# Moving the weight slots and the FFN activations of a two-block transformer kernel by 64 and 128 bytes in SBUF

## The chip, the core and the metric

The kernel runs on one core of a Trainium2 chip. The metric is the device time in microseconds of one execution. Three executions of the kernel before took 1388.61, 1388.72 and 1394.03 us; their median, 1388.72 us, is the time before.

## What is computed

Two transformer blocks run one after the other on 512 tokens with 1024 features, all in fp32. What matters here are the linears, the products of an activation with a weight matrix; everything between them is named only.

```python
def first_block(x, c, ctx, ...):                 # one layer
    h  = modulate(rmsnorm(x), shift, scale)      # 512 x 1024
    hc = modulate(rmsnorm(ctx), ...)             # 256 x 1024
    z  = h @ w_in                                # q, k, v, gate and conv inputs
    kvc = hc @ w_in[:, ATT_W:3 * ATT_W]          # keys and values of the context
    y  = concat(neighbourhood attention, spatial gating, conformer conv) @ w_out
    x  = x + mod[2] * y
    h2 = modulate(rmsnorm(x), ...)
    gate, up = split(h2 @ w_up)                  # 2 x 2816 columns
    x  = x + mod[5] * ((silu(dwconv(gate)) * up) @ w_down)

def second_block(x, ...):                        # one layer
    proj = rms_norm(x) @ w_in                    # q, k, v, conv inputs, gates
    merged = sigmoid(g_att) * (stick_breaking(q, k, v) @ w_att) \
           + sigmoid(g_conv) * (conv branch @ w_conv)
    x = x + rms_norm(merged @ w_out)
    a, g = split(causal_dwconv(rms_norm(x) @ w_up))   # 2 x 2816 columns
    return x + rms_norm((gelu(g) * a) @ w_down)
```

## The kernel before

Activations lie in SBUF with the features on the 128 partitions: `h_hi[:, k, :]` holds the features 128 k to 128 k + 127 of all 512 tokens. Each fp32 operand of a linear is split into a high and a low part in the type fp32r, and a product is three matmuls that add up in one PSUM bank: high weight by high activation, low weight by high activation, high weight by low activation. `product` (with `with_high`, L586 and L587, and `with_low`, L590) issues them. A block of 128 output features is a loop of `product` over the 8 (or, down in the FFNs, 22) chunks of 128 input features. In the trace these matmuls have the lines L586, L587 and L590, whoever calls.

In the call `e.matmul(dst, lhs, rhs)` the second operand is stationary: an instruction of its own, LDWEIGHTS, loads its 128 columns into the array. The third is the moving operand, streamed through with 512 columns, or 256 where half of the tokens are done at a time. In nearly all linears the weight is stationary and the activation moves. It is the other way round where the values are computed with tokens on the partitions: `values_high` and `values_low` (L750, L753, L761) at the start of block one, and the loop over `W["v2"]` in block two (through `product`). There the weight moves.

The weights pass through three slots. SyncE loads a tile of 128 x 1024 fp32 to `raw_w`; ScalarE rounds it to `w_hi` (L1347), and VectorE subtracts to get `w_lo` (L1916). From the second out-projection to the start of the second FFN six further slots, `late_hi` and `late_lo`, are in use as well. The order of the matmuls on TensorE is written out by hand (`mixer_order`, `stick_order`, then plain loops), and so is the order on the other engines; semaphores couple them. Each engine runs its list in order.

The tiles are laid into SBUF one after another in the order of the `sb(...)` lines in `two_blocks`. An inner `with` gives its room back at its end, so the tiles of different stages share addresses. A tile starts at the next multiple of 32 bytes. The first, `x_res`, starts at 16512 bytes of each partition, which is 128 modulo 256. All chunks within the tiles below are whole multiples of 512 bytes apart, so a tile's start modulo 256 is also that of each operand taken from it. Starts, in bytes of a partition:

| tile | stage | start before | modulo 256 |
|---|---|---|---|
| `h_hi`, `h_lo` | all | 32896, 49280 | 128, 128 |
| `raw_w`, `w_hi`, `w_lo` | all | 82752, 95040, 107328 | 64, 64, 64 |
| `hc_hi`, `hc_lo` | mixer of block one | 190176, 198368 | 224, 224 |
| `a_hi`, `a_lo` | first FFN, down | 123904, 168960 | 0, 0 |
| `att_hi`, `att_lo`, `cnv_hi`, `cnv_lo` | merge of block two | 119680, 127872, 136064, 144256 | 128 |
| `m_hi`, `m_lo` | second out-projection | 168832, 185216 | 128, 128 |
| `late_hi`, `late_lo` | between the stages of block two | 119680, 144256 | 128, 128 |
| `a2_hi`, `a2_lo` | second FFN, down | 119680, 164736 | 128, 128 |
| `sp_hi`, `sp_lo`, `minus` | sums of the stick-breaking attention | 203648, 213888, 224128 | 128 |

The trace names both `a_hi` and `a2_hi` as `a_hi`; the first stands at 521 to 646 us, the second at 1254 to 1378 us.

Of the kernel before, what the change touches and what calls it, by code (L numbers as in the profile page):

```python
# [13 lines left out]
P = 128  # L14
D = 1024
KC = D // P
# [25 lines left out]
EPS = 1e-6  # L42
NEG = -1e30
SLOT = 1024


COLUMN_SIZES = [
# [45 lines left out]
class Loads:  # L93
# [5 lines left out]
    def row(self):  # L99
        self.load.append(("row", self.io["ada_rows"][self.n_rows, :, :], SLOT, self.n_rows))  # L100
        self.n_rows += 1
# [171 lines left out]
def two_blocks(nc, io, out):  # L273
    with ExitStack() as whole:
        def sb(stack, name, shape, dt=F32):
            return stack.enter_context(nc.sbuf_tensor(name, shape, dt))
# [19 lines left out]
        both_gains = sb(whole, "both_gains", [P, KC])  # L296
        std = sb(whole, "std", [P, 2 * TT])
        rstd = sb(whole, "rstd", [P, 2 * TT])
        raw = sb(whole, "raw_w", [P, RAW, SLOT])
        w_hi = sb(whole, "w_hi", [P, KEPT, SLOT], F32R)  # L300
        w_lo = sb(whole, "w_lo", [P, KEPT, SLOT], F32R)
        silu_c = sb(whole, "silu_c", [P, KC, 2])
        banks = whole.enter_context(nc.psum_tensor("banks", [P, 8, T], F32))
        bank = [banks[:, b, :] for b in range(8)]
        score_banks, turned_banks = banks[:, 0:2, :], banks[:, 2:4, :]
# [1 line left out]
        with ExitStack() as modulated:  # L307
            silu_row = sb(modulated, "silu_row", [P, D])
            mod_raw = sb(modulated, "mod_raw", [P, 4 * KC])
            with ExitStack() as mixer:  # L310
                mods = sb(mixer, "mods", [P, KC, 4])
                gains = sb(mixer, "gains", [P, KC, 2])
                k_loc = sb(mixer, "k_loc", [P, AC, T])
                k_ctx = sb(mixer, "k_ctx", [P, AC, CTX])
                v_loc = sb(mixer, "v_loc", [P, CBLK, ATT])
                cv_acc = sb(mixer, "cv_acc", [P, CC, T])
                stats = sb(mixer, "stats", [P, 5 * TT])
                sg_square = sb(mixer, "sg_square", [P, SG])
                cv_scratch = sb(mixer, "cv_scratch", [P, CC, T])
                soft = sb(mixer, "soft", [P, 2, 6])  # L320
                group_std = sb(mixer, "group_std", [P, CC * TT * 2])
                group_factor = sb(mixer, "group_factor", [P, CC * TT * 2])
                with ExitStack() as beginning:
                    early = sb(beginning, "early", [P, 6, 2, SLOT])
                q_loc = sb(mixer, "q_loc", [P, AC, T])
                v_mid = sb(mixer, "v_mid", [P, CBLK - 1, ATT])
                v_ctx = sb(mixer, "v_ctx", [P, CT, ATT])
                sg_out = sb(mixer, "sg_out", [P, SC, T])
                sg_v = sb(mixer, "sg_v", [P, TT, SG])
                cv_in = sb(mixer, "cv_in", [P, CC, T + 2 * PAD])  # L330
                sg_small = sb(mixer, "sg_small_sb", [P, SC * P + 2 * SG + 4 * P])
                hc_hi = sb(mixer, "hc_hi", [P, KC, CTX], F32R)
                hc_lo = sb(mixer, "hc_lo", [P, KC, CTX], F32R)
                with ExitStack() as context:
                    xc = sb(context, "xc", [P, KC, CTX])
                with ExitStack() as attention:
                    biased = sb(attention, "biased", [P, 2, len(SPAN_OFFS), 2, SPAN // GROUP, ROWS, GROUP])
                    probs_more = sb(attention, "probs_more", [P, 2, T])
            with ExitStack() as ffn:
                a_hi = sb(ffn, "a_hi", [P, FC, T], F32R)  # L340
                a_lo = sb(ffn, "a_lo", [P, FC, T], F32R)
        with ExitStack() as branch:
# [20 lines left out]
        with ExitStack() as between_stages:  # L363
            late_hi = sb(between_stages, "late_hi", [P, LATE_KEPT, SLOT], F32R)
            late_lo = sb(between_stages, "late_lo", [P, LATE_KEPT, SLOT], F32R)
# [2517 lines left out]
```

## Time and profile before

| | |
|---|---|
| time, median of three | 1388.72 us |
| the profiled execution, first to last instruction (span) | 1387.9 us |
| TensorE busy with matmuls | 1358.3 us, 98% |
| TensorE loading weights (beside the matmuls) | 1123.6 us, 81% |
| VectorE busy | 757.9 us, 55% |
| ScalarE busy | 604.9 us, 44% |
| mean DMA rate | 108 GB/s |
| mean granted TensorE clock | 0.995 of full |

The profile gives the span of the execution that it was taken on, not that execution's own device time; the span is 0.8 us below the median of the time. A matmul that follows another begins before the first one has ended, so the busy time of a group of matmuls, and the mean of one, hold an overlap. How fast a stretch of matmuls goes is read from their starts: the start of the last less the start of the first, by the number of steps between them.

### The profile page before, as it was taken

Reading aid. Unit: us, or ns where it says so; the run is one execution under the profiler, and the core shown is the slowest. Engines: PE = TensorE matmul, PEld = TensorE weight load, DVE = VectorE, ACT = ScalarE, POOL = GpSimd, SP = SyncE. Lnnn points to the kernel's source line nnn. Section 1 sums busy time; section 2 is a strip of 40 time slices with the busy share of each in tenths; the row PEclk is TensorE's granted clock in tenths of the full one; section 3 lists DMA queues with packets and bytes.
Section 4 is the critical chain, followed back from the end, with each engine's and each line's share of the span. In section 5 each row is a group of like instructions: output and inputs, shape, how many; then the busy total and the mean of one; then the engine's idle time right before and its main releaser. Section 6 shows DMA issues by size and latency. Waiting matters only on the chain.

```text
span 1387.9 us, 17388 instructions
## 1 busy us (share of the span) xinstructions
PE 1358.3 (98%) x7040; PEld 1123.6 (81%) x7040; DVE 757.9 (55%) x1070; ACT 604.9 (44%) x866; POOL 4.0 (0%) x11
## 2 busy tenths in 40 slices
PE   5999999999999999999999999999999999999997
PEld 3787877888888888889888888788998788888887
DVE  5679866775554442336414444345777756663224
ACT  5647778453333333224344454334534434443221
POOL 0000000000000000000000000000000000000000
PEclk9999999999999999999999999999999999999998
DMA  9734322414433232332222211234302332223331
GB/s 378 279 129 147 141 73 75 145 64 150 160 113 106 91 95 90 87 107 78 97 86 76 77 61 54 77 103 144 126 1 91 107 103 95 91 87 101 96 97 61
DMA packets 43102, 150.45 MB, mean 108 GB/s; under 512 B 4752, under 2 KB 6928, under 8 KB 41872
## 3 DMA queue, kind: packets, MB, share of 16 engines
q1 hardware_dynamic: 42144, 144.76, 31.2%
q0 software_dynamic: 880, 4.59, 1.0%
q8 instruction: 56, 0.92, 0.3%
q14 instruction: 22, 0.18, 0.0%
HBM read 146.45 MB, written 2.10 MB: 107 GB/s over the span
## 4 chain that ended last, share of the span: by engine, by line
PE 91%; DVE 5%; ACT 2%; issue 1%; DMA 0%; SPq 0%; ACTq 0%; DVEq 0%
PE banks L586 27%; PE banks L587 26%; PE banks L590 26%; DVE w_lo L1916 1%; PE banks L893 1%; ACT w_hi L1347 1%; PE banks L750 1%; PE banks L753 1%; PE banks L761 1%; PE banks L876 1%; PE banks L1157 1%; PE banks L1156 1%; PE banks L1148 1%; PE banks L1184 1%; PE banks L723 1%
## 5 line engine op out<-in xcount | busy, mean ns | idle before, releaser
L586 PE MATMUL banks<-h_hi,w_hi 128*128 128x512 f32 (+1 forms) x1248 | 472.9, 381 | 1.9 <-DVE w_lo L1916 1.3
L587 PE MATMUL banks<-h_hi,w_lo 128*128 128x512 f32 (+1 forms) x1248 | 466.5, 375 | 0.0
L590 PE MATMUL banks<-h_lo,w_hi 128*128 128x512 f32 (+1 forms) x1248 | 461.0, 376 | 0.9 <-DVE h_lo L2271 0.2
L1916 DVE TENSOR_TENSOR w_lo<-raw_w,w_hi 128x1024 fp32r<-128x1024 f32 (+2 forms) x221 | 256.3, 1162 | 321.5 <-ACT w_hi L1347 319.5
L1347 ACT ACTIVATE w_hi<-raw_w 128x1024 fp32r<-128x1024 f32 (+2 forms) x221 | 221.5, 1004 | 231.8 <-PE banks L590 213.4
L586 PEld LDWEIGHTS banks<-h_hi,w_hi 128*128 128x128 f32 x1248 | 234.5, 188 | 50.3 <-issue 6.1
L590 PEld LDWEIGHTS banks<-h_lo,w_hi 128*128 128x128 f32 x1248 | 230.9, 188 | 48.8 <-DVE h_lo L2271 1.9
L587 PEld LDWEIGHTS banks<-h_hi,w_lo 128*128 128x128 f32 x1248 | 234.6, 188 | 40.9
L586 PE MATMUL banks<-a_hi,w_hi 128*128 128x512 f32 (+1 forms) x396 | 146.2, 369 | 0.0
L587 PE MATMUL banks<-a_hi,w_lo 128*128 128x512 f32 (+1 forms) x396 | 146.2, 369 | 0.0
L590 PE MATMUL banks<-a_lo,w_hi 128*128 128x512 f32 (+1 forms) x396 | 145.2, 367 | 0.0
L586 PEld LDWEIGHTS banks<-a_hi,w_hi 128*128 128x128 f32 x396 | 74.4, 188 | 13.8
L590 PEld LDWEIGHTS banks<-a_lo,w_hi 128*128 128x128 f32 x396 | 74.4, 188 | 13.5
L587 PEld LDWEIGHTS banks<-a_hi,w_lo 128*128 128x128 f32 x396 | 74.6, 188 | 12.8
L1985 DVE SCALAR_TENSOR_TENSOR exact<-banks,cols_sb,exact 128x510 f32<-128x510 f32 (+1 forms) x44 | 32.9, 748 | 38.1 <-ACT exact L1873 37.3
L1985 DVE SCALAR_TENSOR_TENSOR normed<-banks,cols_sb,normed 128x510 f32<-128x510 f32 (+1 forms) x66 | 49.2, 746 | 0.8
L1362 ACT ACTIVATE a_hi<-normed 128x512 fp32r<-128x512 f32 x44 | 27.8, 632 | 46.1 <-DVE normed L2332 29.4
L1979 DVE SCALAR_TENSOR_TENSOR cv_acc<-cv_in,cols_sb,cv_acc 128x512 f32<-128x512 f32 x60 | 45.0, 749 | 1.2
L1873 ACT ACTIVATE exact<-banks,cols_sb 128x512 f32<-128x512 f32 x22 | 15.1, 685 | 59.9 <-PE banks L590 59.9
L1646 ACT ACTIVATE normed<-normed 128x512 f32<-128x512 f32 x22 | 13.9, 632 | 54.7 <-DVE normed L2328 54.7
L2440 DVE SCALAR_TENSOR_TENSOR sp<-banks,sp 128x1024 f32<-128x1024 f32 (+1 forms) x8 | 11.9, 1492 | 41.5 <-ACT sp L1738 41.5
L1877 ACT ACTIVATE exact<-exact 128x512 f32<-128x512 f32 x22 | 13.9, 632 | 44.2 <-DVE exact L1985 44.2
(315 smaller groups left out, 1513.7 us busy)
## 6 DMA issues: line engine op xcount, KB each, us to landing
raw_w<-in_w_ffn_up SPq DMA_DIRECT2D x44, 512.0 KB, 3.4
raw_w<-in_w_up SPq DMA_DIRECT2D x44, 512.0 KB, 3.4
raw_w<-in_ada_rows SPq DMA_DIRECT2D x24, 512.0 KB, 3.9
early<-in_ada_turned SPq DMA_DIRECT2D x8, 1024.0 KB, 16.8
raw_w<-in_w_gates SPq DMA_DIRECT2D x16, 512.0 KB, 3.2
raw_w<-in_w_ffn_down SPq DMA_DIRECT2D x16, 448.0 KB, 3.3
raw_w<-in_w_down SPq DMA_DIRECT2D x16, 448.0 KB, 3.3
raw_w<-in_w_conv SPq DMA_DIRECT2D x12, 512.0 KB, 3.3
```

The costliest lines, as they stand in the source:

```text
L586: e.matmul(dst, lhs_hi, rhs_hi, start=first, stop=False)
L587: e.matmul(dst, lhs_lo, rhs_hi, start=False, stop=False)
L590: return e.matmul(dst, lhs_hi, rhs_lo, start=False, stop=last)
L723: done = e.matmul(bank[b][32 * part:32 * part + 2, 0:2 * P], silu_c[:, 2 * m + part // 2, :], tiles[:, half, part * 2 * P:(part + 1) * 2 * ...
L1347: e.activation(hi[:, 0:n], raw[:, i % RAW, 0:n], ACT.Copy).then_inc(s_hi, 1)
L1362: e.activation(dst, src, ACT.Copy).then_inc(done, 1)
L1646: e.activation(y, y, ACT.Silu).then_inc(s_up_silu, 1)
L1873: e.activation(dst, bank[b[n]][:, :], ACT.Copy, scale=col("conv_ffn_w_2", w)).then_inc(s_up2_centre.sem, 1)
L1877: e.activation(y, y, ACT.Gelu_apprx_tanh).then_inc(s_up2_gelu.sem, 1)
L1916: e.tensor_tensor(lo[:, 0:n], raw[:, i % RAW, 0:n], hi[:, 0:n].bitcast(F32), ALU.subtract).then_inc(s_lo, 1)
L1979: e.scalar_tensor_tensor(out=acc, in0=src, scalar=col("cv_w", i), in1=acc, op0=ALU.mult, op1=ALU.add).then_inc(s_tap_v, 1)
L1985: return e.scalar_tensor_tensor(out=y[:, shift:T], in0=src[:, 0:T - shift], scalar=w, in1=y[:, shift:T], op0=ALU.mult, op1=ALU.add)
```

## The change

The small tile `silu_c` (64 bytes) moves from behind `w_lo` to ahead of `raw_w`. Two tiles that nothing uses are put in as gaps: 160 bytes ahead of `hc_hi`, and 128 bytes ahead of `a_hi`. No instruction is added, removed or reordered on any engine; what differs are addresses.

```diff
+BEFORE_A, BEFORE_HC = 32, 40
...
         rstd = sb(whole, "rstd", [P, 2 * TT])
+        silu_c = sb(whole, "silu_c", [P, KC, 2])
         raw = sb(whole, "raw_w", [P, RAW, SLOT])
         w_hi = sb(whole, "w_hi", [P, KEPT, SLOT], F32R)
         w_lo = sb(whole, "w_lo", [P, KEPT, SLOT], F32R)
-        silu_c = sb(whole, "silu_c", [P, KC, 2])
...
                 sg_small = sb(mixer, "sg_small_sb", [P, SC * P + 2 * SG + 4 * P])
+                sb(mixer, "before_hc", [P, BEFORE_HC])
                 hc_hi = sb(mixer, "hc_hi", [P, KC, CTX], F32R)
                 hc_lo = sb(mixer, "hc_lo", [P, KC, CTX], F32R)
...
             with ExitStack() as ffn:
+                sb(ffn, "before_a", [P, BEFORE_A])
                 a_hi = sb(ffn, "a_hi", [P, FC, T], F32R)
                 a_lo = sb(ffn, "a_lo", [P, FC, T], F32R)
```

The tiles that start elsewhere after it:

| tile | start before, modulo 256 | start after, modulo 256 |
|---|---|---|
| `silu_c` | 119616, 64 | 82752, 64 |
| `raw_w` | 82752, 64 | 82816, 128 |
| `w_hi` | 95040, 64 | 95104, 128 |
| `w_lo` | 107328, 64 | 107392, 128 |
| `hc_hi`, `hc_lo` | 190176, 198368, 224 | 190336, 198528, 128 |
| `a_hi`, `a_lo` | 123904, 168960, 0 | 124032, 169088, 128 |
| `xc`, `biased` (share their room) | 206560, 224 | 206720, 128 |
| `probs_more` | 218848, 224 | 219008, 128 |

All other tiles stay where they are.

## Rows read from the trace of the kernel before

**Rows 1.** The page: the chain that ended last, share of the span by engine.
```profile
PE 91%; DVE 5%; ACT 2%; issue 1%; DMA 0%; SPq 0%; ACTq 0%; DVEq 0%
```

**Rows 2.** Groups by shape on TensorE: line, operation, output<-operands, xcount, busy us, mean ns.
```profile
L586 PE MATMUL banks<-h_hi,w_hi 128*128 128x512 f32 x1072 | 425.0, 396 | 0.8 <-DVE w_lo L1916 0.6 <-issue 0.2
...
L586 PE MATMUL banks<-a_hi,w_hi 128*128 128x512 f32 x308 | 121.3, 394 | 0.0
L586 PE MATMUL banks<-h_hi,w_hi 128*128 128x256 f32 x176 | 47.9, 284 | 1.1 <-DVE w_lo L1916 0.8 <-ACT h_hi L1609 0.3
```

**Rows 3.** Timeline of TensorE (start us, us long): first and last matmul, FFN up.
```profile
296.21 0.40 PE L586 MATMUL banks<-h_hi,w_hi 128*128 128x512 f32 x1
...
521.22 0.39 PE L590 MATMUL banks<-h_lo,w_hi 128*128 128x512 f32 x1
```

**Rows 4.** The same for the down-projection of the first FFN.
```profile
521.45 0.39 PE L586 MATMUL banks<-a_hi,w_hi 128*128 128x512 f32 x1
...
629.01 0.39 PE L590 MATMUL banks<-a_lo,w_hi 128*128 128x512 f32 x1
```

**Rows 5.** The same for the down-projection of the second FFN.
```profile
1254.67 0.39 PE L586 MATMUL banks<-a_hi,w_hi 128*128 128x512 f32 x1
...
1360.19 0.39 PE L590 MATMUL banks<-a_lo,w_hi 128*128 128x512 f32 x1
```

**Rows 6.** The same for the values of block two, where the weight moves.
```profile
694.72 0.39 PE L586 MATMUL banks<-w_hi,h_hi 128*128 128x512 f32 x1
...
716.89 0.40 PE L590 MATMUL banks<-w_lo,h_hi 128*128 128x512 f32 x1
```

**Rows 7.** Out-projection of block two: last stretch from `w_hi`, whole stretch from `late_hi`.
```profile
968.99 0.39 PE L586 MATMUL banks<-m_hi,w_hi 128*128 128x512 f32 x1
...
974.25 0.39 PE L590 MATMUL banks<-m_lo,w_hi 128*128 128x512 f32 x1
974.48 0.40 PE L586 MATMUL banks<-m_hi,late_hi 128*128 128x512 f32 x1
...
985.15 0.39 PE L590 MATMUL banks<-m_lo,late_hi 128*128 128x512 f32 x1
```

**Rows 8.** Start of the second FFN: a tile from `late_hi` at full width, first, tenth, last.
```profile
1039.58 0.40 PE L586 MATMUL banks<-h_hi,late_hi 128*128 128x512 f32 x1
...
1041.67 0.39 PE L586 MATMUL banks<-h_hi,late_hi 128*128 128x512 f32 x1
...
1044.84 0.39 PE L590 MATMUL banks<-h_lo,late_hi 128*128 128x512 f32 x1
```

**Rows 9.** Sums of the stick-breaking attention, full width, first and last of ten.
```profile
785.95 0.39 PE L1156 MATMUL banks<-sp_hi,minus 128*128 128x512 f32 x1
...
787.99 0.39 PE L1157 MATMUL banks<-sp_lo,minus 128*128 128x512 f32 x1
```

**Rows 10.** The chain at 55 to 60 us: values of block one (start us, us, what).
```profile
56.23 0.93 PE banks L753 x4
```

**Rows 11.** Half width, 256 columns: the out-projection of block two, from `late_hi`.
```profile
985.38 0.28 PE L586 MATMUL banks<-m_hi,late_hi 128*128 128x256 f32 x1
...
995.69 0.28 PE L590 MATMUL banks<-m_lo,late_hi 128*128 128x256 f32 x1
```

**Rows 12.** Half width, 256 columns: the down-projection of the first FFN, from `w_hi`.
```profile
629.24 0.28 PE L586 MATMUL banks<-a_hi,w_hi 128*128 128x256 f32 x1
...
638.66 0.28 PE L590 MATMUL banks<-a_lo,w_hi 128*128 128x256 f32 x1
```

**Rows 13.** The chain at 1039 to 1080 us, by line.
```profile
by line: DVE w_lo L1916 20.7%; DVE exact L1985 17.4%; DVE normed L1985 17.3%; ACT w_hi L1347 15.4%; DVE normed L2633 8.6%; issue 8.0%; ACT exact L1877 7.8%; PE banks L586 2.1%; PE banks L587 1.4%; PE banks L590 1.2%; ACTq L1872 0.3%; ACT a_
```

**Rows 14.** Instructions of one tile, `a_lo`: ns min/median/max, first and last start.
```profile
L2334 DVE TENSOR_TENSOR a_lo<-normed,a_hi x22: 691/693/694, 296.9 to 523.1; 128x512 fp32r<-128x512 f32 x22
L2635 DVE TENSOR_TENSOR a_lo<-normed,a_hi x22: 691/693/695, 1047.9 to 1259.2; 128x512 fp32r<-128x512 f32 x22
```

**Rows 15.** Windows: us, busy (x count) of PE, PEld, DVE, ACT, POOL, clock, DMA share, GB/s; mixer.
```profile
100.00:262.00 162.00, 158.58 (x1066) 126.14 (x1063) 123.23 (x187) 114.04 (x191) 1.06 (x2) 1.00 0.33 114
```

## The prediction, made before the changed kernel ran

> **What bounds the kernel now.** I read the page first. The chain that ended last lies on TensorE for 91% of the span [rows 1], and TensorE is busy 98% of it, VectorE 55% and ScalarE 44% (table above). So the time is, nearly everywhere, the number of matmuls times the step from one to the next. The mean duration of a matmul, 396 ns for `h_hi,w_hi` and 394 ns for `a_hi,w_hi` [rows 2], doesn't tell that step, since neighbours overlap; the timeline does. The reader is to take two starts far apart and divide by the number of steps between, counted from the loops.
>
> In the up-projection of the first FFN 984 matmuls of full width (41 tiles, 8 chunks, 3 products) start between 296.21 and 521.22 us: 225.01 / 983 = 228.9 ns a step [rows 3]. Directly after it, in the down-projection, 462 matmuls (7 blocks, 22 chunks, 3 products) take (629.01 - 521.45) / 461 = 233.3 ns [rows 4]. The down-projection of the second FFN, the same 462 matmuls of the same form, takes (1360.19 - 1254.67) / 461 = 228.9 ns [rows 5]. TensorE waits for nothing in any of them. By the table of starts the moving operand is at 0 modulo 256 in the slow one and at 128 in the fast ones, while the stationary weight is at 64 in all three. Where the weight itself moves, at 64, the step is slow too: (716.89 - 694.72) / 95 = 233.4 ns in the values of block two [rows 6] and 0.93 us for four, about 233 ns, in those of block one [rows 10]. So the start of the moving operand is worth 4.4 ns.
>
> The stationary operand seems to count as well. In the out-projection of block two the same `m_hi` and `m_lo`, at 128, move over weights first from `w_hi` at 64, (974.25 - 968.99) / 23 = 228.7 ns, and then over weights from `late_hi` at 128, (985.15 - 974.48) / 47 = 227.0 ns, its first step of 0.24 us included [rows 7]. The sums of the stick-breaking attention have both operands at 128 and go at (787.99 - 785.95) / 9 = 226.7 ns [rows 9]. The tile from `late_hi` at the start of the second FFN, both at 128 again, goes at (1044.84 - 1041.67) / 14 = 226.4 ns once it has settled, but its first nine steps took 232.2 ns each [rows 8].
>
> **The change, part by part.** No instruction is added or moved on any queue, so no wait changes its place. What changes is the start of some operands. I cost it against the profiled span of 1387.9 us, which is 0.8 us under the median; I take the differences off the median, 1388.72.
>
> Step after the change: every linear gets both operands at 128, the case of [rows 7 to 9]. I take 226.7 ns, the value of [rows 9], between the settled 226.4 and the 227.0 with its slow first step.
>
> (a) Weight stationary, moving operand already at 128, full width. Chunks: 1072 of `h` and 154 of `a2`, half of the 308 in [rows 2], and by the loops 32 of `att`, 32 of `cnv` and 24 of `m`, together 1314, or 3942 matmuls. Each goes from 228.9 to 226.7, 2.2 ns less. Two stretches are set apart. In the mixer of block one (176 of these chunks, 528 matmuls, worth 1.2 us) TensorE is busy 158.6 of 162 us, but softmax on ScalarE and VectorE (114 and 123 us busy) is part of the chain [rows 15]; short runs between small matmuls may also never settle. I take half, 0.6 us, between 0 and 1.2. From 1045 to 1079 us (34 / 0.2289 = about 149 matmuls, 0.3 us) the chain runs through VectorE and ScalarE, TensorE's lines having a few per cent [rows 13]: a faster TensorE only waits there, and I take nothing. The rest, 3942 - 528 - 149 = 3265, gives 3265 x 2.2 = 7.2 us.
>
> (b) First FFN, down-projection, full width: 462 x (233.3 - 226.7) = 3.0 us.
>
> (c) Values, where the weight moves: 96 matmuls in block two and 144 in block one: 240 x 6.6 = 1.6 us.
>
> (d) Half width. The step of `late_hi` in the out-projection is (995.69 - 985.38) / 86 = 119.9 ns [rows 11], that of `w_hi` in the first FFN (638.66 - 629.24) / 80 = 117.8 ns, with `a` at 0 [rows 12]. So here both at 128 is the slower pair, by 2.1 ns. 176 chunks of `h` [rows 2], 88 of `a` and 32 of `hc` by the loops are 888 matmuls: 888 x 2.1 = 1.9 us more. Between 0, if the half width of `late_hi` is slow for its own reasons, and 2.9 us, if some of the stretches go faster than the one shown.
>
> (e) ScalarE, VectorE and DMA. `a_lo` is written at 0 modulo 256 in the first FFN and at 128 in the second, in 691/693/694 and 691/693/695 ns [rows 14]. So VectorE doesn't see the phase, and I put `raw_w`, `w_lo` and `biased` at nothing. The loads run ahead of their use nearly everywhere; at most the 0.3 us stretch above could show a difference.
>
> Sum: 0.6 + 7.2 + 3.0 + 1.6 - 1.9 = 10.5 us. **Forecast: 1388.7 - 10.5 = 1378.2 us.** Its own ends: with the whole mixer and no half-width loss 13.0 us, 1375.7; with nothing in the mixer, 227.0 ns instead of 226.7 (4400 matmuls x 0.3 = 1.3 us) and 2.9 us lost at half width, 7.6 us, 1381.1.
>
> **The rivals.** *Only the moving operand counts.* The 2 ns between `w_hi` and `late_hi` would then belong to something else that the stretch of `late_hi` has, and full-width steps end at 228.9. What speaks for it is that the big, clean pair [rows 4, 5] shows only the moving operand, and that the slow opening in [rows 8] stands where both are at 128. Against it: in [rows 7] nothing but the weight's place changes from one matmul to the next, and [rows 9] agree in another stage. It gives (462 + 240) x 4.4 = 3.1 us: 1385.6.
>
> *Places don't matter at all*, the change doesn't do what it says: the 4.4 ns between the two down-projections would come from their stages (the FFNs differ in what ScalarE and VectorE do beside them), and the time stays at 1388.7. Against it, [rows 6, 10] are slow in two further stages and share only the place of their moving operand.
> The Trainium skill, page "TensorE: Matmul & The Clock Gate", section "Step-by-step: what each phase is for", says that TensorE has two independent read ports, so that loading the next weights takes nothing from the running matmul, and the page's step for 512 columns is 215.7 ns with no term for an address. By that rule, this rival holds. The trace doesn't bear it out: the same form takes 228.9 ns in one stage and 233.3 in another.
>
> *Slower: the slow opening lasts.* The first nine steps of [rows 8] have `h` moving at 128 over a weight at 128, which is just what 3216 matmuls (1072 chunks) become. If that pair keeps its 232.2 ns instead of settling, those lose 3.3 ns each, 10.6 us, and half width 1.9 us, against 462 x 1.1 = 0.5 us from (b), 240 x 1.1 = 0.3 us from (c) and 726 x 2.2 = 1.6 us from `a2`, `att`, `cnv` and `m`: 10.1 us slower, 1398.8. Between the two paces lie 3216 x 5.5 = 17.7 us, so it decides from a share of 10.5 / 17.7, about six in ten, of those matmuls at the slow pace. Against it: the opening follows directly on half-width matmuls, was over after nine steps, and the long runs in [rows 4, 5] hold one pace.
>
> **How the numbers follow.** Forecast 0.65; only the moving operand 0.15; no effect 0.09; slower 0.07; and 0.04 for a gain beyond my ends. The predicted time is that of the likeliest, 1378.2 us. The range holds the forecast's ends and the first rival, 1375.0 to 1386.5 us, and leaves out the others, 0.20 together. A measurement of this kernel can tell about 0.5%, 6.9 us, from no change, so faster is below 1381.8: the forecast and what lies beyond it, less a few cases at its upper edge, 0.69. Slower is above 1395.7, 0.07. The rest, 0.24, is within 0.5%.
>
> **What the profile of the changed kernel would show.** If I am right: the FFN up-projections go from 228.9 to about 226.7 ns a step, the two down-projections become equal, also at 226.7 (the first from 233.3), the values of block two likewise, the half-width stretches go to about 119.9, and `late_hi` stays where it is. The stretch 1045 to 1079 us keeps its length, with TensorE waiting a little more. The forecast is wrong if `h` over `w` stays at 228.9 (the first rival) or goes to 232 (the last), if the first down-projection stays at 233.3 (places don't matter), or if the steps shorten and the span doesn't, with new waits of TensorE for `w_lo`.

## The result

The changed kernel took 1380.94 us, the median of six executions between 1378.10 and 1383.61, against 1389.81 us (1386.97 to 1394.03) for the kernel before, measured beside it. The ratio is 0.9936, with a 95% interval of 0.9917 to 0.9955: 8.9 us faster. Put on another chip later, beside the kernel before again, it took 1377.98 us against 1389.00, a ratio of 0.9919 (0.9905 to 0.9932), 11.0 us faster. The forecast was 1378.2 us, 10.5 us faster.

The profiled execution of the changed kernel took 1383.48 us, at the slow end of its six, with a span of 1382.2 us. Its page has the same number of instructions, and TensorE is busy for 5.4 us less than before:

```profile
span 1382.2 us, 17388 instructions
## 1 busy us (share of the span) xinstructions
PE 1352.9 (98%) x7040; PEld 1129.3 (82%) x7040; DVE 757.4 (55%) x1070; ACT 604.8 (44%) x866; POOL 4.0 (0%) x11
```

The lines that answer to [rows 3 to 7] are in the timeline of TensorE of the changed kernel (start us, us long, line, operands). All line numbers are three higher than before. First and last matmul of the first FFN's up-projection, of its down-projection, of the values of block two, and of the second FFN's down-projection:

```profile
295.68 0.40 PE L589 MATMUL banks<-h_hi,w_hi 128*128 128x512 f32 x1
...
518.52 0.39 PE L593 MATMUL banks<-h_lo,w_hi 128*128 128x512 f32 x1
518.75 0.39 PE L589 MATMUL banks<-a_hi,w_hi 128*128 128x512 f32 x1
...
623.25 0.39 PE L593 MATMUL banks<-a_lo,w_hi 128*128 128x512 f32 x1
```
```profile
688.96 0.39 PE L589 MATMUL banks<-w_hi,h_hi 128*128 128x512 f32 x1
...
710.49 0.39 PE L593 MATMUL banks<-w_lo,h_hi 128*128 128x512 f32 x1
```
```profile
1249.73 0.39 PE L589 MATMUL banks<-a_hi,w_hi 128*128 128x512 f32 x1
...
1354.22 0.39 PE L593 MATMUL banks<-a_lo,w_hi 128*128 128x512 f32 x1
```

The steps are 222.84 / 983 = 226.7 ns (before 228.9), 104.50 / 461 = 226.7 (233.3), 21.53 / 95 = 226.6 (233.4) and 104.49 / 461 = 226.7 (228.9). All four have become the step of the sums of stick-breaking [rows 9]. Half width went the other way, to the step of [rows 11]; the first FFN's down-projection again, which answers to [rows 12], now takes 9.59 / 80 = 119.9 ns instead of 117.8:

```profile
623.47 0.28 PE L589 MATMUL banks<-a_hi,w_hi 128*128 128x256 f32 x1
...
633.06 0.28 PE L593 MATMUL banks<-a_lo,w_hi 128*128 128x256 f32 x1
```

Cut at the starts of the stages, and at the end at the first of TensorE's last four matmuls (1379.38 and 1373.69 us), the two traces give this ledger, in us:

| stage | before | after | difference |
|---|---|---|---|
| start, values of block one | 66.33 | 65.92 | -0.41 |
| mixer of block one | 196.21 | 195.87 | -0.34 |
| end of out-projection, norm, start of up (half width) | 33.67 | 33.89 | +0.22 |
| first FFN, up | 225.24 | 223.07 | -2.17 |
| first FFN, down, full width | 107.79 | 104.72 | -3.07 |
| its end and norm (half width) | 36.19 | 36.41 | +0.22 |
| queries and keys of block two | 29.29 | 29.08 | -0.21 |
| values, stick-breaking, conv | 180.86 | 179.26 | -1.60 |
| merge | 82.40 | 81.60 | -0.80 |
| second out-projection, full width | 27.40 | 27.24 | -0.16 |
| its end, output norm (half width) | 22.31 | 23.89 | +1.58 |
| output norm, start of up (half width) | 31.89 | 35.38 | +3.49 |
| second FFN, up | 215.09 | 213.40 | -1.69 |
| second FFN, down, full width | 105.74 | 104.72 | -1.02 |
| end (half width) | 18.97 | 19.24 | +0.27 |
| sum | 1379.38 | 1373.69 | -5.69 |

The sum agrees with the spans, 1387.9 and 1382.2 us. Two stages got longer by 5.1 us together, and most of that isn't the places. There the granted clock fell to half, 1.2 of 2.4 GHz. The windows of the kernel before, then of the changed one (us; busy us and instructions of PE, PEld, DVE, ACT, POOL; granted clock; DMA):

```profile
998.00:1002.00 4.00, 4.00 (x22) 4.00 (x23) 1.56 (x8) 1.32 (x4) 0.00 (x0) 0.57 0.01 4
```
```profile
990.00:996.00 6.00, 6.00 (x29) 6.00 (x30) 2.40 (x10) 1.32 (x4) 0.00 (x0) 0.50 0.01 3
1007.00:1013.00 6.00, 6.00 (x29) 6.00 (x29) 4.63 (x18) 1.57 (x5) 0.00 (x0) 0.50 0.01 3
```

The kernel before had one fall of 3.4 us there, the changed one two of 6.8 us. Executions without one show the stages undisturbed: `w_only` (below), with the weights at 128, takes 20.82 and 32.34 us in them, `a_only`, with the weights at 64, 31.89 us in the second. So the falls cost 22.31 - 20.82 = 1.5 us before and (23.89 - 20.82) + (35.38 - 32.34) = 6.1 us after, and the places themselves cost 0.45 us. Without the clock's part the ledger sums to -5.69 - (6.1 - 1.5) = -10.3 us. Executions at the same mean granted clock say nearly the same. On the chip of the second comparison, at 0.995, three of the changed kernel took 1377.85 to 1378.56 us and eleven of the kernel before 1387.94 to 1389.80, their medians 10.8 us apart.

### The profile page after: what moved, and what is told of

It reads as the page before. It is cut to its first block, busy times and chain, and to the rows that moved or that the text cites. A ratio compares the mean times of both kernels' runs of the same rounds, so it can differ in the third digit from the quotient of the medians.

```text
span 1382.2 us, 17388 instructions
## 1 busy us (share of the span) xinstructions
PE 1352.9 (98%) x7040; PEld 1129.3 (82%) x7040; DVE 757.4 (55%) x1070; ACT 604.8 (44%) x866; POOL 4.0 (0%) x11
## 4 chain that ended last, share of the span: by engine, by line
PE 91%; DVE 5%; ACT 2%; issue 1%; DMA 0%; SPq 0%; ACTq 0%; DVEq 0%
PE banks L589 27%; PE banks L593 26%; PE banks L590 26%; DVE w_lo L1919 1%; PE banks L896 1%; ACT w_hi L1350 1%; PE banks L879 1%; PE banks L764 1%; PE banks L756 1%; PE banks L753 1%; PE banks L1160 1%; PE banks L1159 1%; PE banks L726 1%; PE banks L1151 1%; PE banks L1187 1%
```

## The experiments

Twelve runs, on three chips, each beside the kernel before: ten kernels, and once more the change and `after_spread`. `w_96`, `w_160` and `w_lo_off` have two executions each, the others four to twelve.

| kernel | median, us | before, us | ratio (95%) | moving less stationary, modulo 256: `h` over `w`, `a` over `w` |
|---|---|---|---|---|
| `w_only` | 1380.75 | 1389.34 | 0.9935 (0.9913, 0.9957) | 0, 128 |
| `a_only` | 1387.26 | 1389.34 | 0.9980 (0.9968, 0.9992) | +64, +64 |
| `hc_only` | 1388.74 | 1389.34 | 0.9990 (0.9979, 1.0000) | +64, -64 |
| `all_at_192` | 1380.63 | 1389.34 | 0.9925 (0.9901, 0.9949) | 0, 0 |
| `w_96` | 1405.94 | 1389.60 | 1.0117 (1.0092, 1.0142) | +32, -96 |
| `w_160` | 1405.25 | 1389.60 | 1.0112 (1.0089, 1.0135) | -32, +96 |
| `after_spread` | 1377.97 | 1389.60 | 0.9916 (0.9900, 0.9931) | 0, 0 |
| `before_spread` | 1387.10 | 1389.60 | 0.9984 (0.9974, 0.9994) | +64, -64 |
| `before_plus_64` | 1389.01 | 1389.00 | 1.0001 (0.9992, 1.0010) | +64, -64 |
| `w_lo_off` | 1404.74 | 1389.00 | 1.0111 (1.0093, 1.0130) | 0 and -32, 0 and -32 |
| `after_again` | 1377.98 | 1389.00 | 0.9919 (0.9905, 0.9932) | 0, 0 |
| `after_spread_again` | 1377.00 | 1389.00 | 0.9910 (0.9897, 0.9924) | 0, 0 |

### Each part of the change alone

`w_only` is the kernel before with `silu_c` moved:

```diff
+        silu_c = sb(whole, "silu_c", [P, KC, 2])
         raw = sb(whole, "raw_w", [P, RAW, SLOT])
...
-        silu_c = sb(whole, "silu_c", [P, KC, 2])
```

> Only the three weight slots move, from 64 to 128 modulo 256; hc stays at 224 and a at 0. If the weight's place counts (my theory), h over w goes from 228.9 to 226.7 ns a step at full width, the second down-projection likewise, the values with the weight moving from 233.3 to 226.7, half width from 117.8 to 120, and the time falls by 7.2 + 0.6 + 1.6 - 1.9 = 7.5 us before what a does. The first down-projection, a at 0 over w at 128, is a pair not seen yet: 233.3 if the moving operand off 128 is slow whatever the weight does, 226.7 if the weight alone sets it. If only the moving operand counts, h over w stays at 228.9 and the time falls by about 1 us.

Measured: 8.6 us faster. `h` over `w` steps at 226.7 ns (983 steps in 222.85 us), the second down-projection at 226.7. The pair that no trace had shown, `a` at 0 over `w` at 128, stayed slow, (626.51 - 518.95) / 461 = 233.3 ns:

```profile
518.95 0.40 PE L586 MATMUL banks<-a_hi,w_hi 128*128 128x512 f32 x1
...
626.51 0.39 PE L590 MATMUL banks<-a_lo,w_hi 128*128 128x512 f32 x1
```

So the weight's place counts, and most of the gain is in this one 64-byte move: not all of the 8.6 us, though. The profiled execution of `w_only` has no fall of the clock in the output norms, the one of the kernel before has one, worth 1.5 us. Stage by stage, without that, the two traces are 7.1 us apart, where 7.5 were expected. The rival "only the moving operand counts" falls: no `h` moved here.

`a_only` has just the gap ahead of `a_hi`:

```diff
+                sb(ffn, "before_a", [P, 32])
                 a_hi = sb(ffn, "a_hi", [P, FC, T], F32R)
```

> Only a_hi and a_lo move, from 0 to 128; the weight slots stay at 64. By my theory the first down-projection becomes the pair of the second, 228.9 ns a step instead of 233.3: 462 x 4.4 = 2.0 us faster, and all other stretches stay as before. If what slows the first down-projection is its stage and not its place, it stays at 233.3.

As expected, the first down-projection stepped at (628.70 - 523.18) / 461 = 228.9 ns, the step of the second [rows 5], and the time fell by 2.1 us:

```profile
523.18 0.39 PE L587 MATMUL banks<-a_hi,w_hi 128*128 128x512 f32 x1
...
628.70 0.39 PE L591 MATMUL banks<-a_lo,w_hi 128*128 128x512 f32 x1
```

That settles the rival "places don't matter": the stage is the same, the place alone changed. The Trainium skill (page "TensorE: Matmul & The Clock Gate", section "Step-by-step: what each phase is for") says that loading the next weights takes nothing from the running matmul, and it has no cost for an address. Such a cost is there: one and the same stage steps at 228.9 or at 233.3 ns by where its operands lie. Whether it is the weight load that disturbs the matmul, no run here shows.

`hc_only` has just the gap ahead of `hc_hi`:

```diff
+                sb(mixer, "before_hc", [P, 40])
                 hc_hi = sb(mixer, "hc_hi", [P, KC, CTX], F32R)
```

> Only hc_hi and hc_lo move, from 224 to 128 (and xc, biased and probs_more with them). By my theory hc over w at half width, some 96 matmuls at 117.4 ns a step, stays within 3 ns of that, the values with the context stay at 233.3 because their weight still moves at 64, and the time doesn't move: within 0.5 us of before. If the softmax is sensitive to the place of biased or probs_more, the mixer (100 to 262 us) changes by over 0.5 us.

The two medians are 0.6 us apart, which the interval (0.9979 to 1.0000) can't tell from nothing. As expected, `hc` over `w` at half width stays within 3 ns (117.8 ns a step, 117.4 before), and the values with the context stay at 233.4. In the trace the mixer is 0.06 us longer, the start 0.08 and the end 0.09 us shorter, and every other stage is within 0.02 us. The softmax didn't notice.

### Is it the place, or the distance?

In the traces before these runs every fast pair had both operands at 128. `all_at_192` is the whole change plus a gap of 64 bytes ahead of the first tile, so that everything starts at 192.

```diff
+        sb(whole, "before_x", [P, 16])
         x = sb(whole, "x_res", [P, KC, T])
```

> All that the change does, and every tile of the kernel 64 bytes further: the operands of all linears start at 192 modulo 256. If only the distance between the moving and the stationary operand counts (my theory, formed on the traces: distance 0 gives 226.7), every full-width stretch goes at 226.7 ns and half width at 120, as at 128, and the time is that of the change, some 9 to 10 us below before. If 128 itself is the good place of the moving operand (0 and 64 were slow), the full-width stretches go at 229 to 233 ns, and the time is at or above that of before.

It steps at (517.60 - 294.76) / 983 = 226.7 ns, and the time is that of the change:

```profile
294.76 0.40 PE L589 MATMUL banks<-h_hi,w_hi 128*128 128x512 f32 x1
...
517.60 0.39 PE L593 MATMUL banks<-h_lo,w_hi 128*128 128x512 f32 x1
```

The number 128 has nothing to it; what counts is that moving and stationary operand start at the same place modulo 256. `before_plus_64` is the same test for the pair +64: the kernel before with the gap of 64 bytes ahead of `x_res` and nothing else.

> The kernel before with every tile 64 bytes further: h at 192, the weight slots at 128, a at 64 modulo 256, all distances as before. If only the distance counts (my theory), every stretch repeats before: h over w 228.9 ns a step (+64), the first down-projection 233.3 (-64), the values 233.3, and the time is that of before within 1 us. If the places themselves count, h at 192 over w at 128 gives another step than 228.9; after all_at_192 only the pair +64 is open to this.

It repeats before: 1389.01 against 1389.00 us, and 228.9, 233.3 and 228.9 ns in the three FFN stretches.

### The other distances

`w_96` and `w_160` put the weight slots 32 bytes to either side of `h`. Gaps ahead of and behind the slots add up to 256 bytes, so that the tiles behind keep their places modulo 256; `a` stays at 0.

```diff
+        silu_c = sb(whole, "silu_c", [P, KC, 2])
+        sb(whole, "before_w", [P, 56])        # w_160: [P, 8]
         raw = sb(whole, "raw_w", [P, RAW, SLOT])
...
+        sb(whole, "behind_w", [P, 8])         # w_160: [P, 56]
```

> The weight slots start at 96, h, att, cnv, m and a2 at 128, a at 0 modulo 256: distances of the moving from the stationary operand of +32 and, for a, +160 (which is -96). If the step grows with the distance to either side (my theory), h over w lies between 226.7 and 228.9 ns, and a over w near 233.3. If only an equal start gives 226.7 and every other one is a step of its own, h over w is at 228.9 or 233.3. Half width: 120 if it goes with 226.7, 113 to 118 if not. Time between that of w_only, about 8 us below before, and before.

> The weight slots start at 160, h and the others at 128, a at 0 modulo 256: distances of -32 and, for a, +96. By my theory h over w lies between 226.7 (distance 0) and 233.3 (distance -64), and a over w between 228.9 and 233.3. If a positive distance is always 228.9 and a negative one always 233.3, h over w is at 233.3, so that the time rises by some 3942 x 4.4 = 17 us over before, and a over w is at 228.9.

My theory, a step that grows with the distance, fell. 32 bytes off is as bad as 128: `h` over `w` steps at (528.17 - 298.80) / 983 = 233.3 ns in `w_96` (below), and at 233.3 in `w_160` too. The time rose by 16 us in both, 3942 matmuls by 4.4 ns being 17.

```profile
298.80 0.40 PE L588 MATMUL banks<-h_hi,w_hi 128*128 128x512 f32 x1
...
528.17 0.39 PE L592 MATMUL banks<-h_lo,w_hi 128*128 128x512 f32 x1
```

Together, full width, by the distance of the moving from the stationary operand modulo 256:

| distance | step, ns | seen in |
|---|---|---|
| 0 | 226.7 | the change, `w_only`, `all_at_192`, [rows 7, 9] |
| +64 | 228.9 | [rows 3, 5], `a_only`, `before_plus_64` |
| +32, -32, +96, 128 | 233.3 | `w_96`, `w_160`, `w_only` |
| -64 | 233.3 | [rows 4, 6], `before_plus_64` |
| -96 | 234.3 | `w_96`, first FFN down |

These are the long runs; short ones between other matmuls go 1 to 3 ns slower. 256 is the period as far as these kernels show: `m_hi` less `late_hi` is 49152 bytes, a multiple of 512, `w_hi` less `h_hi` in the change 62208, an odd multiple of 256, and both pairs step at 226.7 ns, while a distance of 128 gave 233.3. So the kernel before stood, with most of its matmuls, at the second-best distance. Why +64 is better than the others I can't say.

`w_lo_off` asks whether each matmul pays for its own pair. It is the whole change with 32 bytes between `w_hi` and `w_lo`, and 224 behind.

```diff
         w_hi = sb(whole, "w_hi", [P, KEPT, SLOT], F32R)
+        sb(whole, "before_w_lo", [P, 8])
         w_lo = sb(whole, "w_lo", [P, KEPT, SLOT], F32R)
+        sb(whole, "behind_w", [P, 56])
```

> The whole change, but w_lo alone starts at 160 modulo 256, 32 bytes off the activations; w_hi stays at 128. A distance of 32 bytes gave 233.3 ns a step with both halves of the weight off. If each matmul pays for its own pair of operands (my theory), one in three pays: (2 x 226.7 + 233.3) / 3 = 228.9 ns a step, and the time is some 9 us above the change. If one pair out of place upsets the whole stream, all steps are at 233.3. If the rounding is coarser than one matmul, it stays at 226.7.

I was wrong: with one weight in three off, the mean step is that of all three off, (526.90 - 297.54) / 983 = 233.3 ns, and the time is 15.7 us above before. One step of 233.3 after two of 226.7 would have given 228.9. The single steps in that stretch are 239, 229 and 232 ns in turn, so none of the three kept 226.7.

```profile
297.54 0.40 PE L590 MATMUL banks<-h_hi,w_hi 128*128 128x512 f32 x1
...
526.90 0.40 PE L594 MATMUL banks<-h_lo,w_hi 128*128 128x512 f32 x1
```

In this stream one operand in three out of place was enough for the full loss. It isn't so everywhere: in the values of block two of the same trace, where the weight moves, the 95 steps took 22.02 us, 231.8 ns each, between the two. What in the chip does this the runs don't show.

Half width has no such clean table. Distance 0 gives 119.9 ns in the long runs; the others gave 116.8 (+32), 117.4 (-96), 117.8 (-64 and +64), 118.4 (-32), 118.8 (128) and, as slow as distance 0, 120.0 (+96: 80 steps in 9.60 us in `w_160`). And at +64 one stretch, the first 66 half-width matmuls at the end of the second down-projection, took 117.8 ns a step in the kernel before and (1365.94 - 1358.57) / 65 = 113.4 ns in `a_only`, where that stage is the same:

```profile
1358.57 0.28 PE L587 MATMUL banks<-a_hi,w_hi 128*128 128x256 f32 x1
...
1365.94 0.28 PE L591 MATMUL banks<-a_lo,w_hi 128*128 128x256 f32 x1
```

### The clock in the output norms

In the output norms TensorE adds up squares over the partitions: a row of matmuls with one column, 2.6 us long, twice (L1227, at 996 and 1011 us of the kernel before). Of the eleven profiles of kernels that have these rows in one piece, nine show the clock falling 2.2 to 4.1 us after the start of one of them; `w_only` and `a_only` don't. `after_spread` deals the row out: the running totals are summed ahead, the last parts behind, with a product between any two pieces.

```diff
+            def output_piece(half, what, last_part):
...
+                part = (parts_of if last_part else totals)[what]
...
-                    if (u, j) == (KC, 4):
-                        output_sums(0)
+                    if u == KC and 1 <= j <= 6:
+                        output_piece(0, (j - 1) % 3, j >= 4)
...
-            side_by_side_halves(0, tiles, ..., {1: output_sums, 5: output_spreads})
+            side_by_side_halves(0, tiles, ...,
+                                {(0, 1): output_pieces((CROSS, False), (SCALED_SQUARES, False)),
+                                 (1, 0): output_pieces((Y_SQUARES, False), (Y_SQUARES, True)),
+                                 (1, 1): output_pieces((CROSS, True), (SCALED_SQUARES, True)), 5: output_spreads})
```

`before_spread` is the kernel before with the same edit. Both ran once, and the change with and without it once more.

> The whole change, and the sums over partitions of the output norms (24 matmuls of one column in a row, 2.6 us, twice) are dealt out in pieces of 0.4 to 0.9 us between the products around them. The granted clock fell to half 1 to 3 us after such a row in the traces of before (998 to 1002 us) and of the change (989 to 997 and 1006 to 1014 us), and the stretch of the output norms was 1.5 us longer for the first and 6.1 us for the second than in executions without it. If the rows of one-column matmuls bring the clock down (my theory), the clock stays at 1.00 from 985 to 1035 us, the runs lie close together at 1377.0 to 1378.5, and the median is 2 to 4 us below that of the change. If the clock falls for another reason, the median stays at 1380.9 and the runs spread over 5 us as before.

> The kernel before with its one-column matmuls dealt out in the same way. By my theory the clock stays at 1.00 in the output norms and the median falls by 2 us to about 1387.0, with runs close together; the difference to after_spread is then the change without the clock's part: by stage the two traces give 10.7 us. If the change costs clock drops that the kernel before does not have, the difference of these two is larger than that of the change and before (8.9 us); if the drops have nothing to do with it, it is the same 8.9 us.

> The change once more, beside after_spread_again on the same chip: median 1380.9, runs in groups at 1378, 1381 and 1383.5 us by how often the clock fell in the output norms.

> The change with its one-column matmuls dealt out, once more, for the interval: 1377 to 1379 us, below after_again by 2 to 4 us. If the first run of it was luck, the two have the same median.

In all three profiles with the edit the clock stays at 1.00 through the output norms. Windows of `after_spread_again`, then of `after_again`, which has the row in one piece:

```profile
977.00:998.00 21.00, 21.00 (x179) 20.96 (x179) 14.50 (x37) 9.56 (x23) 0.00 (x0) 1.00 0.18 62
998.00:1030.00 32.00, 32.00 (x272) 32.00 (x271) 22.94 (x67) 8.71 (x20) 0.00 (x0) 1.00 0.01 1
```
```profile
976.00:997.00 21.00, 21.00 (x179) 20.96 (x179) 15.38 (x39) 9.56 (x23) 0.00 (x0) 1.00 0.21 73
997.00:1030.00 33.00, 33.00 (x268) 33.00 (x267) 22.83 (x67) 8.63 (x20) 0.00 (x0) 0.95 0.00 1
```

The kernel before fell by 2.5 us, from 1389.60 to 1387.10, as expected. `after_spread` took 1377.97 us, its four between 1377.12 and 1378.75: 3.0 us below the change's 1380.94, but that was on another chip. The five executions of `after_spread_again` lie between 1376.53 and 1377.31 us, close together as expected. But `after_again` didn't repeat the 1380.9 that I expected: its four lie between 1377.32 and 1378.56, so the edit was worth 1.0 us on that chip, not 2 to 4. How often the clock falls differs between sets of executions, and the edit doesn't end all falls: four of twelve executions of `before_spread` were at 1388.9 to 1389.5 us and a clock of 0.994, the other eight at 1386.2 to 1387.7 and 0.997 or 0.998. No profile caught one of the four, so where their clock fell is open. The output norms aren't the only place: in all but one profile (`before_spread`) it is at half for 3.4 or 6.8 us between 20 and 29 us, and in `a_only` for 3.4 us at 208 us, right after 16 matmuls of two columns (205.9 to 207.9 us), which made the mixer 1.6 us longer.

Between the two kernels with the edit, on one chip, the change is worth 1387.10 - 1377.97 = 9.1 us; between the two without, 8.9 and 11.0 us by chip. My expectation that the 8.9 of the first comparison would either stay or grow can't be decided by these numbers: `after_spread` had a mean clock of 0.995 or 0.996, most of `before_spread` 0.997. At the same clock, 0.997, four executions of `after_spread_again` and seven of `before_spread` have medians 10.1 us apart, though on two chips. The 10.7 us in that expectation came of cutting the last stage at the fourth of four matmuls before and at the first of them after; cut alike, it is 10.3. The best version is the change with the rows dealt out, 1377.00 us, 0.9910 (0.9897 to 0.9924) of before.

## Why the prediction was right

The forecast, 1378.2 us, lies 2.7 us below the first median and 0.2 us above the one of `after_again`; the way, the mechanism and most terms were right. That the sum of 10.5 us comes so near to the ledger's 10.3 is partly luck: (d) charged 0.7 us too much, and (c) and the mixer promised 0.8 us too much.

- **What bounds the kernel**: right. The time followed the step of the matmuls, stage by stage, and no new wait appeared. What the prediction took for the place of the moving operand ("worth 4.4 ns") is its distance from the stationary one: `all_at_192` and `before_plus_64` show that the place doesn't matter.
- **(a) Weight stationary**: expected 7.2 us outside the mixer. The ledger has 2.17 + 0.21 + 0.80 + 0.16 + 1.69 + 1.02, and of the 1.60 the 0.96 that aren't values: 7.0 us. The 226.7 ns came from the nine steps of [rows 9], between 226.4 and 227.0 in 14 and 47 others [rows 8, 7], and held for thousands. In the mixer I took 0.6 us, and 0.34 came. The stretch that I left out kept its length: it ends with TensorE's wait for `w_lo`, which grew by what TensorE had gained. Before and after (the idle time in brackets):

```profile
1078.76 0.50 PE L586 MATMUL banks<-h_hi,w_hi 128*128 128x512 f32 x1 [0.57 <-DVE w_lo L1916]
```
```profile
1075.49 0.50 PE L589 MATMUL banks<-h_hi,w_hi 128*128 128x512 f32 x1 [0.90 <-DVE w_lo L1919]
```

  From the `late_hi` tile of [rows 8] to that wait's end it is 1078.76 - 1039.58 = 39.18 us before and 1075.49 - 1036.33 = 39.16 after.
- **(b) First down-projection**: expected 3.0 us, 3.07 came.
- **(c) Values**: in block two 95 steps went from 22.17 to 21.53 us, 0.64 as expected. In block one I had 1.0 us and the two traces show 0.41. Its last 72 matmuls gained 0.47 us, as priced (from 49.54 to 66.33 us before, from 49.60 to 65.92 after); the earlier ones, in pieces between others, show no gain in these two traces, with the clock at half for 3.4 us in both. That stage starts behind the first loads and varies: it ends at 64.9 to 66.1 us in the traces with the weights in line with `h` and at 65.4 to 66.5 in those with them at the distance of before. The averages, over six and five traces, are 0.6 us apart.
- **(d) Half width**: mis-sized. The step was right, 119.9 ns, but I charged 2.1 ns for all 888 matmuls, 1.9 us. The ledger has +0.22, +0.22, (without the clock) +0.45 and +0.27, 1.2 us. Many of these matmuls stand side by side with a norm and wait for their inputs, and there the longer step is hidden, just as the shorter one was in the stretch above: the 45 from 272 us and the 102 from 282 us on go at 153.3 and 139.8 ns a step before and at 153.1 and 140.3 after. I hadn't taken those off.
- **(e) Other engines**: right. `a_lo` in the changed kernel takes 691/693/695 ns in the first FFN, as in [rows 14].
- **The slow opening** [rows 8] stayed an opening: the runs of 984 matmuls hold 226.7.

What the sum didn't have is the clock. I worked from differences of steps at full clock, which give the 10.3 us of the ledger. The times of the first set go with the clock: 1378.1 and 1378.2 us at a mean of 0.995, 1380.9 and 1381.0 at 0.993, 1383.5 and 1383.6 at 0.991 and 0.990, and their median is one at 0.993: against the 10.3 to 10.8 us at an equal clock, 1.4 to 1.9 us are lost to it. The clocks of the kernel before in that set are not on record but for the profiled execution's 0.995. Whether the change has a part in the falls is open. In the second set, with the changed kernel at 0.995 and 0.997, the two were 11.0 us apart.

## What to carry to other kernels

Where matmuls with a weight load each run back to back, check where their operands start in SBUF: all moving and stationary operands of a stream at the same place modulo 256 bytes gave 226.7 ns a step, nearly every other arrangement 233.3. A small tile allocated ahead of a large one can so cost or give 2% of a matmul-bound kernel: this one took 1378 us with all operands in line and 1405 with the weights 32 bytes off. Read the step from starts far apart, not from the mean duration; pairs that occur in different stages of one trace are then experiments already made. And before a difference of under 1% is put down to an edit, look at the granted clock in both traces, window by window.

## What the runs showed of the hardware

- In long runs the step of full-width fp32r matmuls with a weight load each takes few values: 226.7, 228.9 and 233.3 ns (once 234.3). 32 bytes of distance cost as much as 128, and with one operand in three out of place all three steps were slower than 226.7 (`w_lo_off`: 239, 229 and 232 ns).
- The distance modulo 256 counts, not the place, as far as a shift of 64 bytes shows: the kernel before 64 bytes further, with its distances of +64 and -64, took the same time (1389.01 and 1389.00 us) and the same steps, and so did the change at 192 instead of 128 (226.7 ns).
- At half width the equal start is among the slowest, 119.9 ns, with 120.0 at +96 and 113.4 to 118.8 elsewhere. And there one stretch at the same distance has two paces: 117.8 and 113.4 ns at +64, and near 640 us, at -64, steps of 117 to 119 ns in two traces (`hc_only`, `before_plus_64`) and of 113 to 114 in two (before, `before_spread`).
- The granted clock fell to half, in nine of eleven profiles, in or after a row of one-column matmuls in which TensorE had no idle gap: the windows above show it busy all through, by a profile that models where a matmul ends. The Trainium skill (page "TensorE: Matmul & The Clock Gate", section "HAM oscillation — how this bites in real kernels") tells of the clock falling over idle gaps; in these stretches the trace shows none. The fall came 2.2 to 4.1 us after the start of the row. It cost 1.5 us where it lasted 3.4 us and about 3 us where it lasted 6.8 us.
